# The last loads of two HGRN weights, split into sixteen transfers of 15 to 1 and 8 rows

## The reference: what is computed

```
for i in range(DEPTH):                       # DEPTH = 2
    xn = rmsnorm(h, mixer_norm[i])
    if i % N_MIXERS == 0: h = h + swa_attention(xn, attn_w_in, attn_sinks, attn_w_out)
    else:                 h = h + hgrn2(xn, hgrn_w_in, lb, hgrn_out_norm, hgrn_w_out)
    h = h + peer_ffn(rmsnorm(h, ffn_norm[i]), peer_w_q[i], peer_sub_keys[i], peer_u[i], peer_v[i])
return rmsnorm(h, final_norm)

# peer_ffn, per token: 8 heads choose 16 of 16384 experts each
u = u_tab[expert]                            # 128 rows of 1024 for each token
act = gelu(einsum('pd,phkd->phk', xb, u))
out = einsum('phk,phkd->pd', gates * act, v_tab[expert])
# hgrn2: q, f, i, g = split(xn @ w_in, 4), a gated recurrence over chunks, a norm, then @ w_out
```

## Time and profile before

| what | value |
|---|---|
| time, median of 3 runs | 1486.58 us (1485.42 to 1487.67) |
| profiled execution, span from the first to the last instruction | 1485.0 us |
| the median less that span | 1.6 us |
| busy: PE / DVE / ACT / POOL | 1283.3 / 1087.0 / 612.0 / 598.9 us |
| moved by DMA | 603.45 MB, mean 406 GB/s |

### The profile page before, as it was taken

How to read it: one execution, slowest core, us unless ns; L and a number is a source line. 1 busy time by engine, 2 the same in 40 slices (tenths; PEclk the granted TensorE clock), 3 DMA queues, 4 the chain that set the end, 5 groups by cost and what they waited for, 6 DMA issues and landing times.

```text
span 1485.0 us, 15450 instructions
## 1 busy us (share of the span) xinstructions
PE 1283.3 (86%) x4728; PEld 708.4 (48%) x4728; DVE 1087.0 (73%) x2659; ACT 612.0 (41%) x1826; POOL 598.9 (40%) x521
## 2 busy tenths in 40 slices
PE   8997987978978899898997799988999688978777
PEld 5664544434545556464454465645445344422222
DVE  3479887965788788797589778778759877675444
ACT  3344344443443343343455335234455443443334
POOL 0134455443444333343444434334444454434442
PEclk9999999999999999999999999999999999999999
DMA  9499999999999999999999999999999999999996
GB/s 369 179 402 421 419 421 421 421 421 422 415 422 420 405 416 402 422 420 416 421 422 420 422 404 402 410 423 421 420 422 411 423 421 421 421 422 411 421 422 261
DMA packets 83394, 603.45 MB, mean 406 GB/s; under 512 B 9904, under 2 KB 10608, under 8 KB 12016
## 3 DMA queue, kind: packets, MB, share of 16 engines
q0 software_dynamic: 74016, 536.90, 87.5%
q1 hardware_dynamic: 8576, 65.05, 10.7%
q10 hardware_dynamic: 720, 0.52, 0.1%
HBM read 601.39 MB, written 1.05 MB: 406 GB/s over the span
## 4 chain that ended last, share of the span: by engine, by line
DMA 45%; PE 33%; DVE 11%; ACT 6%; issue 4%; POOL 1%; DVEq 0%; POOLq 0%
DMA ring<-experts,idx 44%; PE acc L1533 19%; DVE ring L1121 6%; PE rbank L1483 3%; PE ab L1405 2%; PE ab L1408 1%; ACT diag L566 1%; PE acc L1262 1%; ACT coef L566 1%; PE y L1273 1%; ACT L677 1%; POOL ring L546 1%; DVE h L1132 1%; DMA ring<-attn_in 1%; ACT gel L677 1%
## 5 line engine op out<-in xcount | busy, mean ns | idle before, releaser
L1533 PE MATMUL acc<-ring,diag 128*128 128x512 f32 x1772 | 874.5, 620 | 186.9 <-ACT diag L566 175.1
L546 POOL DMA_INDIRECT ring<-experts,idx x510 | 592.6, 1162 | 808.3 <-PE acc L1533 670.9
L1121 DVE CUSTOM_DVE_ANT_0 ring<-ring,xn 128x1024 f32<-128x1024 f32 x512 | 626.0, 1224 | 273.4 <-DMA ring<-experts,idx 265.1
L1533 PEld LDWEIGHTS acc<-ring,diag 128*128 128x128 f32 x1772 | 313.6, 193 | 569.4 <-ACT diag L566 317.9
L677 ACT ACTIVATE gel<-dots 128x1 f32<-128x1 f32 x512 | 103.7, 203 | 756.7 <-DVE dots L1121 755.3
L566 ACT ACTIVATE diag<-ident,coef 128x128 f32<-128x128 f32 x443 | 178.1, 402 | 14.4
L566 ACT ACTIVATE coef<-gate,gel 128x1 f32<-128x1 f32 x512 | 151.2, 295 | 16.7
L1483 PEld LDWEIGHTS rbank<-xTs,wroute 128*128 128x128 f32 x832 | 112.3, 194 | 54.1 <-issue 53.2
L1483 PE MATMUL rbank<-xTs,wroute 128*128 128x128 f32 x832 | 113.6, 277 | 0.4 <-issue 0.4
L1132 DVE SCALAR_TENSOR_TENSOR h<-ring,coef,h 128x1024 f32<-128x1024 f32 x69 | 88.4, 1282 | 3.6 <-ACT coef L566 2.5
L1405 PEld LDWEIGHTS ab<-xTs,wmix 128*128 128x128 f32 x384 | 50.9, 195 | 12.8 <-issue 12.1
(11 more groups left out here) (290 smaller groups left out, 1022.6 us busy)
## 6 DMA issues: line engine op xcount, KB each, us to landing
wmix<-hgrn_in SPq DMA_DIRECT2D x21, 1024.0 KB
wroute<-route_w SPq DMA_DIRECT2D x8, 2304.0 KB, 15.6
ring<-experts,idx POOLq DMA_INDIRECT x510
wmix<-hgrn_out SPq DMA_DIRECT2D x7, 1024.0 KB
wmix<-attn_out SPq DMA_DIRECT2D x4, 1024.0 KB, 11.0
wroute<-hgrn_in SPq DMA_DIRECT2D x4, 1024.0 KB, 10.6
ring<-attn_in SPq DMA_DIRECT2D x2, 1536.0 KB, 9.3
ring<-attn_in SPq DMA_DIRECT2D x2, 768.0 KB, 8.2
```

The costliest lines, as they stand in the source:

```text
L546: pool.indirect_dma_start(out=ring[:, k * 2 * D:(k + 1) * 2 * D], out_offset=None, in_=experts, in_offset=bass.IndirectOffsetOnAxis(ap=idx ...
L1121: dve.tensor_tensor_reduce(out=u_rows(k), in0=u_rows(k), in1=xn[:, tile], scale=1.0, scalar=0.0, op0=ALU.mult, op1=ALU.add, accum_out=dots ...
L1533: last = nc.tensor.matmul(acc[:, j * HALF:(j + 1) * HALF], diag[:, m % DIAGS], v_rows(k)[:, j * HALF:(j + 1) * HALF], start=n % PER == 0, ...
```

## The change

The last unit of HGRN's input weights (unit 31) and the last part of its output weights are each written by sixteen transfers in place of one. The transfers take consecutive rows: 15, then 14, 13 and so on down to 1, and then 8, together 128. They are issued back to back on SP, each adds 16 to the same semaphore, and the value that PE waits for is raised by 15 times 16. All other loads, all bytes and all addresses are as before.

```
--- before.py
+++ after.py
@@ -1,3 +1,4 @@
+import itertools
 from contextlib import ExitStack
 
 import numpy as np
@@ -75,6 +76,7 @@
 FOURTH = (Pair(spread((50, 66)), 66, 67, (68,) + spread((70, 73), (75, 80)) + (88,), 85),
           Pair(spread((45, 57)), 57, 58, spread((59, 63)) + (74, 75, 77) + spread((79, 82)), 78),
           Pair(spread((36, 52)), 52, 53, tuple(range(54, 73, 2)), 67))
+STAIR = tuple(range(15, 0, -1)) + (8,)
 FIRST_HEAD_ONE = spread((3, 9)) + (10,)
 LAST_AHEAD = (3, 4, 5, 6)
 HEAD_DVE = {0: tuple(range(111, 118)), 1: (118, 119, 120, 122, 123, 125, 126)}
@@ -367,6 +369,16 @@
         LATE = ((lbr[:], lb_raw), (place[:].rearrange("p c a -> p (c a)"), place_in.to_broadcast([P, 2 * TOPK])), (hmask[:], masks_hgrn),
                 (ogain[:], out_gain))
 
+        def stairs():
+            ends = list(itertools.accumulate(STAIR))
+            return [slice(end - rows, end) for end, rows in zip(ends, STAIR)]
+
+        def stair_load(load):
+            return load == max(m for m in range(32) if m not in UNIT_KEPT)
+
+        def in_place(load):
+            return 16 * loads_into_place(load) + 16 * (len(STAIR) - 1) * stair_load(load)
+
         def win0(g):
             return ring[:, g * AIN:(g + 1) * AIN] if g < ITERS - 1 else wroute[:, 2, 0:AIN]
 
@@ -444,7 +456,12 @@
                     sp.wait_ge(h_proj, last_use_of_place(x) + 1)
                 else:
                     sp.wait_ge(r_score, CHUNKS + (6 if place < UNIT_HOMES + 2 else 5))
-                sp.dma_start(unit_weights(place), hgrn_in[heads_at(tile, i) * 2 + j][:, half * 2 * D:(half + 1) * 2 * D]).then_inc(whgrn_in[place], 16)
+                of = hgrn_in[heads_at(tile, i) * 2 + j][:, half * 2 * D:(half + 1) * 2 * D]
+                if stair_load(x):
+                    for rows in stairs():
+                        sp.dma_start(unit_weights(place)[rows], of[rows]).then_inc(whgrn_in[place], 16)
+                else:
+                    sp.dma_start(unit_weights(place), of).then_inc(whgrn_in[place], 16)
 
             def load_hgrn_out(tile, i):
                 n = tile * ITERS + i
@@ -452,7 +469,11 @@
                     sp.wait_ge(h_outproj, n)
                 else:
                     sp.wait_ge(a_outproj, 2 * ITERS)
-                sp.dma_start(bands(wmix[:, UNIT_HOMES], HH), hgrn_out[heads_at(tile, i)]).then_inc(whgrn_out_in, 16)
+                if n == TILES * ITERS - 1:
+                    for rows in stairs():
+                        sp.dma_start(bands(wmix[:, UNIT_HOMES], HH)[rows], hgrn_out[heads_at(tile, i)][rows]).then_inc(whgrn_out_in, 16)
+                else:
+                    sp.dma_start(bands(wmix[:, UNIT_HOMES], HH), hgrn_out[heads_at(tile, i)]).then_inc(whgrn_out_in, 16)
 
             def load_route(layer, pair):
                 if layer and pair < 2:
@@ -1399,7 +1420,7 @@
                             if step != r % 7:
                                 continue
                             if c == 0 and k == 0:
-                                pe.wait_ge(whgrn_in[place], 16 * loads_into_place(load))
+                                pe.wait_ge(whgrn_in[place], in_place(load))
                             first, end, key = u == 0 and k == 0 and c == 0, u == 1 and k == KT // 2 - 1, half * KT // 2 + k
                             if c < 2:
                                 last = nc.tensor.matmul(ab[:, j, c * P:(c + 1) * P], w[:, k, c * P:(c + 1) * P], xTs[:, 0, key],
@@ -1457,7 +1478,7 @@
                     c, j = (r - 33) // 2, (r - 33) % 2
                     if r == 33:
                         pe.wait_ge(h_oT_ready, n + 1)
-                        pe.wait_ge(whgrn_out_in, 16 * hgrn_out_loads(n))
+                        pe.wait_ge(whgrn_out_in, 16 * hgrn_out_loads(n) + 16 * (len(STAIR) - 1) * (n == TILES * ITERS - 1))
                     last = nc.tensor.matmul(y[:, j * HALF:(j + 1) * HALF], h_oT(tile)[:, c],
                                             wmix[:, UNIT_HOMES, c * D + j * HALF:c * D + (j + 1) * HALF], start=i == 0 and c == 0, stop=True,
                                             skip_group_check=True)
```

## The result

The changed kernel takes **1509.33 us** (median of 4 runs, 1509.11 to 1510.46) against 1486.45 us for the kernel before on the same chip (1485.42 to 1487.67). The ratio is 1.0155, with a 95% interval of 1.0143 to 1.0167: 22.9 us slower. The forecast was 1483.5 us, with a range of 1481.5 to 1490.5, so even the range missed it.

What follows compares the result with a forecast made beforehand. The prediction took the DMA transfers as the limit, with one late engine setting when late gathers land. Its terms, 0 (issue) + 0 (wait) - 3.1 = -3.1 us, against a median of 1486.58 gave 1483.5 us, range 1481.5 to 1490.5.

Steps and rivals of the forecast that it cites:

- the lead of the fifteen: At the end of the gathers, the other fifteen DMA engines finish on average 6.1 us before the last one.
- The transfers are the limit and the engines that compute have slack.: From 1100 to 1400 us, DMA share is 1.01 at 418 to 421 GB/s, while DVE has 86 us free.
- One late engine, 6.1 us behind.: At the end of the gathers one DMA engine works alone, 6.1 us behind the others' mean, setting when late gathers land.
- Issue, 0.: SP's 30 extra issues, 7.1 us for each sixteen, cost 0; without cover 6.8 us for each sixteen.
- Each deals out one row an engine, always from the same first engine.: In both split loads, engines in order carry 16, 15, 14 down to 0 rows of each, in place of 8.
- A row is 8192 B, at one engine's 26.3 GB/s 0.311 us.: Price of a row in both loads; an engine's work changes by 5.0 us at most, either way.
- The late engine at the poor end, -3.1 us.: The late engine gets 0 to about 3 rows of each load, gaining 1.1 to 5.0 us, middle 3.1; chance 0.62.
- rival C: The late engine is at the rich end: sixteen rows of each load cost 5.0 us, giving 1491.6 us; chance 0.15.
- the tail is longer than 4.3 us by up to 5: Sign at the end of the gathers if the late engine has many rows: its time alone grows by up to 5 us.
- the two places that the prediction names: Late engine's place, from engines 7 and 15 being usually slower: it would lose 5.0 us or get 0.6 us more work.
- The wait for the weights, 0.: Unit 31 lands 15.6 us after issue, PE needs it at 17.0 us, 1.4 us to spare, so PE's wait costs 0.
- The share dips as engines without rows go on with gathers only: Sign between 1012 and 1030 us: the DMA share dips, and PE's row of unit 31 doesn't wait.

Runs made afterwards that it cites:

- stair_stride: The changed kernel's sixteen transfer sizes in both loads, but each transfer's rows eight partitions apart; 1501.16 us against 1486.63 for the kernel before.
- block16: Both loads as eight transfers of 16 neighbouring rows, in place of the changed kernel's sixteen; 1502.57 us against 1486.63 for the kernel before.
- src_stride: Eight transfers of 16 rows a load, read eight rows apart in HBM, written to neighbouring partitions; 1502.42 us, ratio 1.0105 to the kernel before.
- stride16: Both loads as eight transfers of 16 rows eight partitions apart, in place of the changed kernel's sixteen; 1495.21 us, ratio 1.0063 to the kernel before.
- dst_stride: Eight transfers of 16 rows a load, read as neighbours from HBM, written eight partitions apart; 1494.28 us against 1486.43 for the kernel before.
- block32: Both loads as four transfers of 32 neighbouring rows, in place of the changed kernel's sixteen; 1493.73 us against 1486.43 for the kernel before.
- rows120_8: Each load as one transfer of 120 rows and one of 8, in place of the changed kernel's sixteen; 1495.12 us against 1485.43 for the kernel before.
- stride32: Both loads as four transfers of 32 rows four partitions apart, in place of the changed kernel's sixteen; 1486.4 us against 1486.43 for the kernel before.
- low8: Each load as two transfers of 32 spread rows and eight of 8, meant to load the first eight engines more; 1491.22 us against 1485.43 before.
- low4: Each load as three transfers of 32 spread rows and eight of 4, meant to load the first four engines more; 1492.92 us against 1485.43 before.
- low2: Each load as 112 spread rows in even transfers and eight transfers of 2, meant to load the first two engines more; 1488.38 us against 1485.43 before.
- cols8: Both loads as eight transfers of all 128 rows, each 1 KB wide, in place of the changed kernel's sixteen; 1491.96 us against 1486.63 for the kernel before.

## Why it came out so: one sum for all kernels

Two terms are taken for each kernel. *Rate:* for both loads, the time of the load times (1 - its GB/s / 421), the bytes that were not moved while it ran. *Tail:* for both loads, the rows over 8 that fall on the engine in the third or fourth place, times the prediction's 0.311 us. For the changed kernel: 24.8 x (1 - 237/421) = 10.8 and 25.6 x (1 - 260/421) = 9.8, together 20.6 us; 14 or 13 rows are 5.5 over 8, x 2 x 0.311 = 3.4 us.

```
kernel         rate   tail   sum    measured   gathers late after loads / later still
changed        20.6   3.4    24.0   22.9       20.9 /  3.1
stair_stride   11.3   3.4    14.7   14.5       11.8 /  2.9
block16        15.5   0      15.5   15.9       15.6 /  0.0
src_stride     15.4   0      15.4   16.0       15.6 /  0.0
stride16        7.8   0       7.8    8.6        7.9 / -0.1
dst_stride      8.7   0       8.7    7.9        8.9 /  0.1
block32         8.4   0       8.4    7.3        8.5 / -0.3
rows120_8       9.3   0.6     9.9    9.7        9.4 /  0.9
stride32        0.3   0       0.3    0.0        1.1 / -0.2
low8            2.6   2.5     5.1    5.8        3.3 /  1.8
low4            3.4   3.7     7.1    7.5        4.0 /  4.2
low2            3.3  -0.6     2.7    2.9        4.7 / -0.5
cols8           2.0   0       2.0    5.3       10.6 / -0.8 (PE waits 12.7 us for unit 31)
```

All are in us over the kernel before. Sum and measured time agree within 1.1 us in every row but cols8. The last column is a second look, from the packets' records of one execution each: the gathers' packets of 8192 B are put in order of start, and the n-th is compared with the n-th of the kernel before. Its first number is how much later they start just behind the second load than they did at 1008 us, the second what came on top by those of 1250 us in the kernel before. Single executions differ in it by about 1 us (stride32: 1.1).

**The two terms show at different times.** The five kernels with even engines and a low rate (block16, src_stride, stride16, dst_stride, block32) lose all of it during the loads and nothing behind them. The two stairs, low8 and low4, whose late engine has more rows, lose 1.8 to 4.2 us more behind the loads, where the tail term has 2.5 to 3.7; low2, whose late engine has fewer, gives 0.5 back. These are the 3 us lost between 1088 and 1160 in the changed kernel. They fit a reason why the lead of the fifteen stayed at 6.4 us: they are held back with the late engine, since POOL issues into a slot only after all rows of an earlier gather have landed and been used. That reason follows from the program and was not tried by a run.

One thing was chosen to fit, the place of the late engine. In the first two places low2 would be 3.3 + 4.4 = 7.7 us, and 2.9 was measured; in the fifth to eighth low4 would be 3.4 - 1.2 = 2.2 us, and 7.5 was measured; in the second half low8 would be 2.6 - 2.5 = 0.1 us, and 5.8 was measured. A packet's record names no engine, but engines can be followed, not without slips, by taking the packet that starts where another ended. Followed so through the second load, they carry 16, 15, 14, 14, 11, 11, 10, 9, 7, 6, 5, 4, 3, 2, 1 and 0 rows, and the one that is last at the end of the kernel carries 13 or 14. That agrees with the fit, but is no proof of the place. The rate term is measured in each run, not derived, so the table shows where the time lies. That crowding of the written places makes the rate is shown by the pairs of kernels, not by the table.

As to what a "place" is, the runs show that 16 neighbours (205 to 210 GB/s in block16) are worse than 16 rows eight apart (272 to 281) or 32 neighbours (252 to 256), and 32 rows four apart are free (402 to 418). The Trainium skill, page "SBUF — State Buffer", section "Door 1: The DMA port swizzle", has 16 ports for DMA; four neighbouring partitions share one, 32 further is the same one, 64 further another. By it these transfers reach 4, 8, 8 and 16 ports. At its 27.2 GB/s a port a row of 8192 B takes 0.301 us. If each row of the load goes with one of a gather, the busiest port has 4 + 1 of every 32 rows in block16, 2 + 1 of 32 in stride16, 4 + 2 of 64 in block32 and 2 + 2 of 64 in stride32, which makes an estimate of 174, 290, 290 and 435 GB/s. The measured rates (205 to 210, 272 to 281, 252 to 256, 402 to 418) agree in size within about a fifth; the estimate has no difference between the middle two. The Trainium skill, page "DMA: Bandwidth & Descriptors", section "The descriptor swizzle", adds that in a transfer to 128 partitions each engine writes one port of its own. By that the whole load and the gathers, and cols8's transfers of 128 partitions too, never have two engines meet at a port, while transfers of fewer rows can. That may be why rows120_8 is slow; how its 15 engines divide the 120 rows no record shows. No row of a trace here names a port or a partition of a packet, so this stays the Trainium skill's account, with which the runs agree.

## The prediction, step by step

**"The transfers are the limit and the engines that compute have slack."** Right. What was lost was lost in the transfers, and PE's long wait in the first load was for a gather.

**One late engine, 6.1 us behind.** Right as a reading (6.4 us after). But it did not follow that its rows set the change alone; the rate of all sixteen sets most of it. A slip beside it: 74016 packets are 514 x 144, but q1's 8576 are 59.6 x 144, no whole multiple, as its transfers have several shapes; nothing in the sum hangs on it.

**Issue, 0.** Right. SP's blocks lasted 5.63 and 5.93 us, not 7.1, and nothing stood behind them.

**"Each deals out one row an engine, always from the same first engine."** Right, as far as packets can be followed: 16, 15, 14 down to 0 rows.

**"A row is 8192 B, at one engine's 26.3 GB/s 0.311 us."** This is the step that failed. It carried the rate of the earlier trace rows, measured with 128-row transfers alone, over to transfers of 15 rows and fewer. In the changed kernel a gather's packet of 8192 B took a median of 521 ns in the first load and 505 in the second, against 313 before. The prediction had no term for it, and none of its rivals did; it is 20.6 us of the sum above, where the prediction's own sum was -3.1 us. As a price for an extra row on one engine, 0.311 us held.

**The late engine at the poor end, -3.1 us.** Wrong in sign. It is third or fourth, with 14 or 13 rows, and the term is +3.4 us. That was rival C, at 0.15; its price was near, its sign ("the tail is longer than 4.3 us by up to 5") did not come (6.4 us after 6.1). Nor is it the eighth or the last in the order, the two places that the prediction names. In the table that place is a fit, the delay behind the loads is not. The stair could only have helped an engine from the ninth place on, and no row told the place: a forecast that hangs on an unread place should have had even chances on either side.

**The wait for the weights, 0.** The wait didn't show, but the working was off: the last packet of the first load ended at 1040.5, 28.2 us after the issue, not 15.6. PE was held by late gathers until 1037.53 and first used unit 31 at 1041.96, 1.5 us behind that packet; that this was just enough is luck. In cols8, where the gathers came through, a load of 24.3 us made PE stand 12.69 us.

**Signs named ahead.** "The share dips as engines without rows go on with gathers only" was wrong as put: the share stays at 1.0 and GB/s falls. A share of 1 says that engines have packets under way, not how fast the bytes move.

## What to carry to other kernels

Beside running 128-row gathers, load weights in transfers of 128 partitions, or, where a load has to be split, in parts that reach across all partitions with the rows left whole, like 32 rows four apart, and not by blocks of neighbouring rows. Read GB/s beside the DMA share in each stretch: full share at half the bytes was here a crowded destination, and it slowed the gathers' queue too, which hadn't changed. Price a transfer of a new shape by a row of that shape, and if the trace has none, keep the range open to the side of a slower rate for everything that runs beside it.

## What was not expected of the hardware

- Two loads of 1 MB, written in blocks of 16 neighbouring rows, held all 16 engines to 205 to 210 GB/s for 15.2 and 15.4 us, gathers included; with rows four apart in blocks of 32 the same bytes ran at 402 to 418 GB/s.
- Splitting off 8 rows of 128 was enough: 241 to 247 GB/s and 9.7 us.
- The engine that is last of the 16 is, by the fit above, the third or fourth in the order in which small transfers are dealt. What sets it apart wasn't tried. In the kernel before a q14 packet of 8192 B is followed by a gather's packet of 968 ns at 1127, 1173, 1235 and 1300 us, in place of 313; the one of 1300 follows onto the late engine, and whether these make it late is open.
- Left open: low8, low4 and low2 cost 0.2 to 0.7 us more than the sum; a packet's port was seen in no trace; why a transfer of 120 rows on 15 engines is slow was not separated from its companion of 8 rows; and the stair on one of the two loads alone was not run.
